# The FFNs' seven-product loop in a new order on VectorE and ScalarE, weight units' low parts on VectorE, and the products' weights 64 bytes off

## The chip, the cores and the metric

One core of one Trainium2 chip runs the whole kernel. The metric is device time in microseconds for one execution; smaller is better.

## The reference, cut to what matters

512 tokens of width 1024 pass through three layers in float32; each layer is a mixer and then an FFN. The mixers (pooling with dilated attention, retention, stick-breaking attention) are not touched by the change. The three FFNs have this form:

```python
def swiglu(h, w_in, w_out):
    gate, up = jnp.split(h @ w_in, 2, axis=-1)
    return (jax.nn.silu(gate) * up) @ w_out
```

The hidden width is 2816, 22 tiles of 128. Around an FFN stand an RMS norm of its input and the addition to the residual x.

## The kernel before, in words

**Products in two parts.** The result has float32 precision. Each float32 operand is split into a high part, rounded to fp32r, and a low part, the rest. A product is then three matmuls: high weights by high input, high by low, low by high. Everything is kept transposed: x is [128, 8 chunks, 512 tokens], and the weights are the stationary operand.

**Weight units.** A unit is the 8 chunks [128, 8, 128] that make one tile of 128 outputs. SP loads it into RAW (two slots, taken in turn), ScalarE (ACT) casts it to WH (`split_hi`, L374), GpSimd (POOL) takes WL = RAW - WH (`split_lo`, L645), and TensorE (PE) runs 16 matmuls of 512 columns on WH (`high_part`, L393 and L394) and 8 on WL (`low_part`, L402). SP starts the load two units on when the low part of a slot has been taken (`s_lo`); ACT's cast waits for the load (`s_raw`) and for PE to have used the slot's high part (`s_hi_used`); `s_unit` counts finished units.

**The FFN's up-projection.** Of the 22 hidden tiles, 14 (NC) are made by plain units, a gate unit and an up unit for each tile, into PSUM banks; VectorE (DVE) scales the gate by the norm RB (`gate_scaled`, L2158), ACT takes its silu, DVE scales the up part (L2162) and multiplies both (L2165). The other 8 (NS) are made by seven products in place of eight, as Strassen and Winograd do it: the 1024 x 2 tiles of weights (gate and up) and the 1024 x 512 input are cut in 2 x 2 blocks, and seven products of block sums (Q1, Q2, Q7, Q6, Q5, Q3, Q4 in the order of PE), each of 12 matmuls of 256 columns (L845, L847, L849), are added up in three half banks: a = B4, b = B5, c = B6. The sums of input blocks (TH, TL) are made once per FFN, those of weight blocks once per group, a group ahead.

**Opening.** PE runs four pairs of units (PRO = 4) while DVE makes the sums of the input (`input_sums`, L2172 to L2191, and their low parts, L2194 and L2198) and the first group's weight sums. In the first FFN the units 0 to 2 run inside the norm's update, and the banks of the pairs are given in the call (L2639). In the others, each pair writes B0 and B1 and so waits for the scaling of the pair before it (L816, L821). At its end DVE gives PE four credits for the banks (`sem_inc(t_bank, 4)`, L2309).

**The loop.** Eight iterations `seven(i)` follow on PE (L857), ACT (L1589) and DVE (L2236), each written out by hand in a fixed order. PE in one iteration: Q1, Q2, Q7, the high part of a gate unit, Q6, its low part, Q5, the high part of an up unit, Q3, Q4, its low part. In between PE waits for the low weights of each product (`t_lo`) and for banks that DVE has read (`t_bank`) or ACT has kept (`t_kept`: ACT copies a's partial sum after Q6 into CW). DVE copies a into GS and adds b (L2239, L2241), scales it (L2243), makes the sums for group i + 1 (L2208, L2212, L2216, L2219) and their low parts (`lo`, L2224), scales the plain gate, copies c into US (L2256) and subtracts a (L2258), which gives a back for Q3, and finishes the hidden tile (L2264 to L2271). ACT starts the loads of the next group's blocks (L1556 into SUMS7, L1557 into R), casts high parts and takes the silus.

**Tail.** The last two pairs of plain units run on PE while ACT and DVE split the finished hidden tiles HD into MH and ML (`some_hidden`; L1620 and L2280), which are the moving operands of the down projection. PE begins that when the last gate has been scaled; its first unit waits for each tile of M (L414 to L419).

**Memory.** Tensors are laid one behind the other in the order in which the code names them; `scratch` gives several lists the same place. A spacer PHASE of 128 bytes ahead of the scratch area makes MH, ML, SH7, SL7, TH and TL start at a multiple of 512 bytes. SH7 and SL7, the high and low weights of the seven products, stand first (each 28 x 128 elements), then TH. IDENT, the identity of the transposes, starts at 384 modulo 512.

## Time and profile before

| | |
|---|---|
| three executions | 2015.53, 2017.98, 2019.43 us; median 2017.98 |
| the profiled execution | 2017.78 us, its span 2016.0 us |
| PE busy | 1956.5 us (97%) in 9919 matmuls |
| DVE, ACT, POOL busy | 1172.7, 873.5, 663.5 us |
| chain that ended last | PE 73%, DVE 17%, DMA 5%, issue 3% |
| mean granted clock of TensorE | 0.992 |

Matmuls are pipelined and their records overlap, so a busy PE is not one at its peak: the distance from start to start says more than a matmul's own duration. A line of the trace has start, duration, engine, line of code, operation, output and inputs, and in brackets the idle time of the engine ahead of it with the instruction that ended it. DVEq is DVE's sequencer (an instruction without arithmetic). A row of a stretch has its bounds and length, each engine's busy time with the instructions in brackets, the granted clock of TensorE as a share of the full 2.4 GHz, the DMA engines' share and GB/s.

### The profile page before, as it was taken

How to read it: one execution, taken by the hardware profiler on the slowest of the kernel's cores; microseconds unless marked ns; L12 is line 12 of the kernel's file. 1: busy time of each engine (PE TensorE's matmuls, PEld its weight loads, DVE VectorE, ACT ScalarE, POOL GpSimd, SP SyncE). 2: the span in 40 equal slices, each digit the busy share in tenths (PEclk: the TensorE clock that was granted, in tenths of full speed). 3: DMA queues.
4: the chain of work that ended last, by engine and by line, in shares of the span. 5: the costliest groups of instructions: out<-in, count | busy, mean ns of one | idle time of the engine just before them, and what ended most of it. 6: DMA issues, size and time to landing. Idle time of an engine off the chain costs nothing.

```text
span 2016.0 us, 28330 instructions
## 1 busy us (share of the span) xinstructions
PE 1956.5 (97%) x9919; PEld 1635.1 (81%) x9919; DVE 1172.7 (58%) x1628; ACT 873.5 (43%) x1251; POOL 663.5 (33%) x259
## 2 busy tenths in 40 slices
PE   9999989999999999999999999999999999999999
PEld 6777778887888888888878888888777777888787
DVE  5765776767137456454277776324778777676600
ACT  6664533334234444434343334225888643232411
POOL 3233331214423334343442123443222243122443
PEclk9999989999999999999999999999999999999999
DMA  5212123222323222222332222322111132322222
GB/s 174 67 63 94 58 100 104 85 71 97 100 85 102 76 94 88 68 94 73 105 125 84 94 83 75 100 96 83 63 52 62 51 115 86 110 88 73 87 97 98
DMA packets 49023, 177.53 MB, mean 88 GB/s; under 512 B 5568, under 2 KB 6464, under 8 KB 48960
## 3 DMA queue, kind: packets, MB, share of 16 engines
q1 hardware_dynamic: 39744, 147.78, 22.2%
q10 hardware_dynamic: 9216, 28.91, 4.2%
q8 instruction: 40, 0.66, 0.1%
q14 instruction: 23, 0.19, 0.0%
HBM read 174.57 MB, written 2.10 MB: 88 GB/s over the span
## 4 chain that ended last, share of the span: by engine, by line
PE 73%; DVE 17%; DMA 5%; issue 3%; ACT 1%; DVEq 1%; ACTq 1%; SPq 0%
PE B L393 16%; PE B L394 16%; PE B L402 15%; DMA R<-in_w_seven 4%; DVE S L2216 3%; DVE HD L2165 2%; PE B L845 2%; DVE SL L2224 2%; PE B L849 2%; PE B L847 2%; DVE ML L2280 2%; PE B L1367 2%; PE B L414 1%; PE B L1175 1%; PE B L419 1%
## 5 line engine op out<-in xcount | busy, mean ns | idle before, releaser
L645 POOL TENSOR_TENSOR WL<-RAW,WH 128x1024 fp32r<-128x1024 f32 (+1 forms) x248 | 652.5, 2633 | 1324.9 <-PE B L402 835.5
L374 ACT CAST WH<-RAW 128x1024 fp32r<-128x1024 f32 (+1 forms) x252 | 278.6, 1107 | 636.0 <-PE B L394 558.5
L393 PE MATMUL B<-HH,WH 128*128 128x512 f32 x1224 | 482.1, 394 | 11.0 <-ACT WH L374 6.2
L394 PE MATMUL B<-HL,WH 128*128 128x512 f32 x1224 | 479.2, 392 | 0.0
L402 PE MATMUL B<-HH,WL 128*128 128x512 f32 x1224 | 304.8, 391 | 0.0
L393 PEld LDWEIGHTS B<-HH,WH 128*128 128x128 f32 x1224 | 231.2, 189 | 61.9 <-issue 8.7
L394 PEld LDWEIGHTS B<-HL,WH 128*128 128x128 f32 x1224 | 231.2, 189 | 46.3
L402 PEld LDWEIGHTS B<-HH,WL 128*128 128x128 f32 x1224 | 226.3, 188 | 45.6 <-POOL WL L645 0.4
L393 PE MATMUL B<-MH,WH 128*128 128x512 f32 x440 | 171.2, 389 | 0.0
L394 PE MATMUL B<-ML,WH 128*128 128x512 f32 x440 | 171.2, 389 | 0.0
L2328 DVE TENSOR_TENSOR X<-X,B 128x512 f32 x26 | 17.9, 687 | 206.7 <-PE B L402 192.9
L2140 DVE TENSOR_TENSOR ACC<-ACC,SQ 128x512 f32<-128x512 f32 x38 | 74.3, 1954 | 108.3 <-ACT SQ L1508 108.2
L845 PE MATMUL B<-HH,SH 128*128 128x256 f32 x288 | 86.5, 300 | 36.5 <-DVE SQ L2258 26.8
L847 PE MATMUL B<-TL,SH 128*128 128x256 f32 x384 | 109.0, 284 | 0.0
L849 PE MATMUL B<-TH,SL 128*128 128x256 f32 x384 | 109.0, 284 | 0.0
L845 PE MATMUL B<-TH,SH 128*128 128x256 f32 x384 | 108.9, 284 | 0.0
L1530 ACT ACTIVATE SG<-G 128x512 f32<-128x512 f32 x42 | 26.5, 631 | 188.5 <-DVE G L2158 188.4
L402 PE MATMUL B<-MH,WL 128*128 128x512 f32 x429 | 103.6, 389 | 0.0
L393 PEld LDWEIGHTS B<-MH,WH 128*128 128x128 f32 x440 | 82.6, 188 | 17.2
L394 PEld LDWEIGHTS B<-ML,WH 128*128 128x128 f32 x440 | 82.6, 188 | 17.1
L845 PEld LDWEIGHTS B<-HH,SH 128*128 128x128 f32 x288 | 57.6, 200 | 47.6 <-DVE SQ L2258 35.6
L402 PEld LDWEIGHTS B<-MH,WL 128*128 128x128 f32 x429 | 80.5, 188 | 16.7
(434 smaller groups left out, 3636.3 us busy)
## 6 DMA issues: line engine op xcount, KB each, us to landing
RAW<-in_w_small SPq DMA_DIRECT2D x206, 512.0 KB, 3.4
RAW<-in_w_large SPq DMA_DIRECT2D x48, 704.0 KB, 4.0
SUMS<-in_w_seven ACTq DMA_DIRECT2D x24, 512.0 KB, 4.0
R<-in_w_seven ACTq DMA_DIRECT2D x24, 512.0 KB, 4.8
out_t<-X SPq DMA_DIRECT2D x7, 256.0 KB, 5.1
X<-in_x_t ACTq DMA_DIRECT2D x4, 256.0 KB, 6.0
X<-in_x_t SPq DMA_DIRECT2D x4, 256.0 KB, 6.3
DECAY<-in_decay ACTq DMA_DIRECT2D x4, 256.0 KB, 2.6
```

What stands on the lines that cost most here:

```text
L374: act.copy(wh, raw).then_inc(s_hi, 1)
L393: pe.matmul(bank, wh[:, c, :], xh[:, k0 + c, :], start=(start and c == 0), stop=False)
L394: mm = pe.matmul(bank, wh[:, c, :], xl[:, k0 + c, :], start=False, stop=False)
L402: mm = pe.matmul(bank, wl[:, c, :], xh[:, k0 + c, :], start=False, stop=(stop and c == chunks - 1))
L645: pool.tensor_tensor(wl, raw, wh.bitcast(F32), ALU.subtract).then_inc(s_lo, 1)
L845: pe.matmul(bank, wh, xh[:, rows.start + c, cols], start=(start and c == 0), stop=False, skip_group_check=True)
L847: pe.matmul(bank, wh, xl[:, rows.start + c, cols], start=False, stop=False, skip_group_check=True)
L849: mm = pe.matmul(bank, wl, xh[:, rows.start + c, cols], start=False, stop=(c == 3), skip_group_check=True)
L1367: mm = pe.matmul(B[bank][:, o:o + w], weights, part[:, h, at:at + w], start=(start and n == 0), stop=(stop and n == 1), skip_group_check=True)
L2140: dve.tensor_tensor(ACC[:], ACC[:], SQ[b][:], ALU.add).then_inc(s_sq_used, 1)
L2165: dve.tensor_tensor(HD[:, i + NS, :], SG[:], U1[:], ALU.mult).then_inc(s_hidden, 1)
L2216: dve.tensor_tensor(S3[:], s6, A12, ALU.add).then_inc(t_sum, 1)
```

## The change

Five things.

1. Memory: TH (and TB22) come ahead of the weights, a spacer of 64 bytes follows (PHASE_SEVEN), then SH7, SL7 and SUMS7, which thus start at 64 modulo 512 bytes; further spacers bring what follows back to 0.
2. The low parts of the units 4 to 27 of every FFN are taken by DVE (`weights`) at written places, no longer by POOL, which waits meanwhile.
3. The loop's order on DVE and ACT; ACT makes the two PSUM copies; the low parts of Q4, Q3, Q6 and Q5 are made in the iteration that uses them.
4. The opening: pairs 1 to 3 of the second and third FFN use the banks (2, 3), (4, 5), (0, 1); the bank credits are given before the weight sums; loads of the first blocks start earlier. In the first FFN unit 7 uses B1.
5. The tail: the split of hidden tiles is spread otherwise.

```diff
-        MH, ML, G1, SG, U1, _, F = scratch([
-            ("MH", [P, FC, T], F32R), ("ML", [P, FC, T], F32R), ("G1", [P, T]), ("SG", [P, T]),
+        MH, _, ML, G1, SG, U1, _, F = scratch([
+            ("MH", [P, FC, T], F32R), ("PAST_MH", [P, 128]), ("ML", [P, FC, T], F32R), ("G1", [P, T]), ("SG", [P, T]),
...
-        SH7, SL7, TH, HD, _, S3, TL, R = scratch([
-            ("SH7", [P, 28, P], F32R), ("SL7", [P, 28, P], F32R), ("TH", [P, 16, T // 2], F32R), ("HD", [P, FC, T]),
+        TH, _, SH7, SL7, _, HD, _, S3, TL, R = scratch([
+            ("TH", [P, 16, T // 2], F32R), ("PHASE_SEVEN", [P, 16]), ("SH7", [P, 28, P], F32R), ("SL7", [P, 28, P], F32R),
+            ("PAST_SL7", [P, 112]), ("HD", [P, FC, T]),
...
POOL
+            by_vector = 2 * NC - 4
...
             for count, chunks in stretches:
+                if not chunks:
+                    first += count
+                    pool.wait_ge(s_lo, first)
+                    continue
...
PE, opening
                     use_unit(pe, Unit(u0 + 6), B[2][:], DC, HH, HL)
-                    pe.wait_ge(s_up, 1)
-                    use_unit(pe, Unit(u0 + 7), B[3][:], DC, HH, HL)
+                    pe.wait_ge(s_up, PRO - 1)
+                    use_unit(pe, Unit(u0 + 7), B[1][:], DC, HH, HL)
                 else:
                     pair(0, before)
-                    for n in range(1, PRO):
-                        pair(n)
+                    pe.wait_ge(s_gate, NC * f + 1)
+                    for n, bank in ((1, 2), (2, 4), (3, 0)):
+                        if n == 3:
+                            pe.wait_ge(s_up, NC * f + 1)
+                        use_unit(pe, Unit(u0 + 2 * n), B[bank][:], DC, HH, HL)
+                        use_unit(pe, Unit(u0 + 2 * n + 1), B[bank + 1][:], DC, HH, HL)
...
PE, loop: Q6 waits for t_lo + 5 (before: + 3), Q5 for + 6 (+ 4), Q3 and Q4 for none
...
ACT, loop
+                    act.wait_ge(t_lo, i * 6 + (6 * group0 + 3))
                     if produce:
-                        products_done(i, 2)
-                        act.wait_ge(t_lo, i * 6 + 6 * (group0 + 1))
-                        load(i + (group0 + 1))
+                        act.dma_start(R[:], blocks[i * 2 + (2 * group0 + 3)]).then_inc(t_landed_2, 16)
+                    products_done(i, 2)
+                    act.copy(GS[:, FIRST], B[5][:, FIRST]).then_inc(t_second, 1)
+                    if produce:
+                        act.dma_start(LANDED_1, blocks[i * 2 + (2 * group0 + 2)]).then_inc(t_landed_1, 16)
+                    products_done(i, 3)
+                    act.copy(US[:, SECOND], B[6][:, FIRST]).then_inc(t_seventh, 1)
                     split_hi(act, Unit(u0 + 2 * PRO + 2, i, 2), DC)
-                    if produce:
-                        singles_hi(ahead)
                     products_done(i, 4)
                     act.copy(CW, B[4][:, FIRST]).then_inc(t_kept, 1)
                     if produce:
+                        singles_hi(ahead)
                         sum_7_hi(ahead)
...
DVE, loop
+                def weights(u):
+                    dve.wait_ge(s_hi, u.index + 1)
+                    dve.wait_ge(s_unit, u.index - 1)
+                    raw, wh, wl = place(u)
+                    dve.tensor_tensor(wl, raw, wh.bitcast(F32), ALU.subtract).then_inc(s_lo, 1)
+
                 def seven(i, produce=True):
                     ahead = i + 1
-                    products_done(i, 2)
-                    dve.tensor_copy(GS[:, FIRST], a).then_inc(t_c11, 1)
-                    dve.wait_ge(t_c11, i * 2 + (2 * group0 + 1))
-                    dve.tensor_tensor(GS[:, FIRST], GS[:, FIRST], b, ALU.add).then_inc(t_bank, 1)
+                    lo(i, 6, Q4, A22)
+                    lo(i, 5, Q3, S3[:])
+                    up_and_hidden(i + (PRO - 1), B[1][:])
+                    dve.wait_ge(t_second, i + (group0 + 1))
+                    dve.tensor_tensor(GS[:, FIRST], GS[:, FIRST], a, ALU.add).then_inc(t_bank, 1)
+                    lo(i, 3, Q6, s6)
+                    weights(Unit(u0 + 2 * PRO, i, 2))
                     dve.wait_ge(t_bank, i * 4 + ((4 * NS + 4) * f + 5))
-                    dve.tensor_tensor(GS[:, FIRST], GS[:, FIRST], RB[:, FIRST], ALU.mult).then_inc(t_c11, 1)
+                    dve.tensor_tensor(GS[:, FIRST], GS[:, FIRST], RB[:, FIRST], ALU.mult).then_inc(t_first_half, 1)
+                    lo(i, 4, Q5, s5)
+                    weights(Unit(u0 + 2 * PRO + 1, i, 2))
...
                         sum_3(ahead)
+                    gate_scaled(i + PRO, B[0][:])
+                    if produce:
                         low_singles(ahead)
-                        lo(ahead, 2, Q7, s7)
-                    gate_scaled(i + PRO, B[0][:])
                     products_done(i, 5)
-                    dve.wait_ge(t_kept, i + (group0 + 1))
-                    dve.tensor_copy(US[:, SECOND], c_).then_inc(t_up, 1)
-                    dve.wait_ge(t_up, i + (group0 + 1))
+                    dve.wait_ge(t_seventh, i + (group0 + 1))
                     dve.tensor_tensor(US[:, SECOND], US[:, SECOND], a, ALU.subtract).then_inc(t_bank, 1)
                     if produce:
                         minus_sum_5()
-                        lo(ahead, 3, Q6, s6)
-                        lo(ahead, 4, Q5, s5)
+                        lo(ahead, 2, Q7, s7)
...
-                    up_and_hidden(i + PRO, B[1][:])
-                    if produce:
-                        lo(ahead, 5, Q3, S3[:])
-                        lo(ahead, 6, Q4, A22)
...
DVE, opening and tail
+                opening_gate(0)
+                opening_up(0)
                 input_sums()
-                opening_pair(1)
+                opening_gate(1)
+                dve.wait_ge(s_lo, u0 + 4)
+                weights(Unit(u0 + 4))
+                opening_up(1)
+                weights(Unit(u0 + 5))
                 input_sums_lo()
-                opening_pair(2)
+                opening_gate(2)
+                weights(Unit(u0 + 6))
+                opening_up(2)
+                dve.sem_inc(t_bank, 4)
                 sum_7(0)
                 sum_6(0)
                 sum_3(0)
                 minus_sum_5()
+                weights(Unit(u0 + 7))
                 low_singles(0)
                 lo(0, 2, Q7, s7)
...
-                opening_pair(3)
-                dve.sem_inc(t_bank, 4)
+                opening_gate(3)
...
+                end = u0 + 2 * (NC - 2)
+                weights(Unit(end))
+                up_and_hidden(NC - 3, B[1][:])
+                weights(Unit(end + 1))
+                some_hidden(range(0, 5))
                 gate_scaled(NC - 2, B[0][:])
-                some_hidden(range(0, 5))
+                weights(Unit(end + 2))
+                some_hidden(range(5, 9))
                 up_and_hidden(NC - 2, B[1][:])
-                some_hidden(range(5, 14))
+                weights(Unit(end + 3))
+                some_hidden(range(9, 12))
                 gate_scaled(NC - 1, B[0][:])
-                some_hidden(range(14, 18))
+                some_hidden(range(12, 19))
                 up_and_hidden(NC - 1, B[1][:])
-                some_hidden(range(18, FC))
+                some_hidden(range(19, FC))
```

ACT's opening loads the first blocks ahead of pair 1, and casts unit 8 between the singles and the sums; its tail follows the same spread of hidden tiles (0 to 4, 5 to 8, 9 to 11, 12 to 18, 19 to 21).

## Rows read from the trace of the kernel before

**Rows 1.** The page's first line.
```profile
span 2016.0 us, 28330 instructions
```

**Rows 2.** The page's groups by line: busy, mean ns of one | idle before, releaser.
```profile
L845 PE MATMUL B<-HH,SH 128*128 128x256 f32 x288 | 86.5, 300 | 36.5 <-DVE SQ L2258 26.8
```

**Rows 3.** Stretches (openings, loops, tails): length, busy PE PEld DVE ACT POOL, PEclk, DMA.
```profile
240.25:272.65 32.40, 21.99 (x81) 16.95 (x80) 29.71 (x42) 17.56 (x27) 9.87 (x5) 0.88 0.24 82
1021.75:1048.58 26.83, 22.53 (x97) 17.86 (x96) 24.77 (x29) 14.81 (x21) 11.83 (x5) 1.00 0.30 102
1657.42:1685.69 28.27, 22.53 (x98) 17.87 (x97) 26.48 (x29) 14.73 (x21) 10.05 (x4) 0.99 0.33 115
272.65:454.08 181.43, 172.86 (x1056) 154.75 (x1057) 119.36 (x164) 54.45 (x82) 39.23 (x16) 0.98 0.27 90
1048.58:1229.51 180.93, 171.74 (x1057) 153.62 (x1057) 119.23 (x164) 54.55 (x82) 39.86 (x16) 0.99 0.27 90
1685.69:1867.60 181.91, 172.88 (x1056) 154.77 (x1057) 119.16 (x164) 54.55 (x83) 39.97 (x16) 0.98 0.26 87
454.08:478.10 24.02, 21.93 (x98) 17.84 (x96) 20.00 (x21) 11.22 (x19) 11.34 (x4) 1.00 0.33 111
1229.51:1253.51 24.00, 21.92 (x97) 17.84 (x95) 19.97 (x21) 11.21 (x19) 11.33 (x4) 1.00 0.34 112
1867.60:1891.60 24.00, 21.92 (x97) 17.84 (x95) 19.99 (x21) 11.21 (x19) 11.34 (x4) 1.00 0.33 113
```

**Rows 4.** Timeline of PE, first matmul of Q3 in the second FFN's third iteration.
```profile
1112.23 0.38 PE L845 MATMUL B<-HH,SH 128*128 128x256 f32 x1 [1.40 <-DVE SQ L2258]
```

**Rows 5.** Timeline of DVE in the same iteration.
```profile
1104.62 0.69 DVE L2208 TENSOR_TENSOR SUMS<-SUMS,R 128x512 f32<-128x512 f32 x1 [4.35 <-DMA R<-in_w_seven]
...
1106.07 2.77 DVE L2216 TENSOR_TENSOR S<-SUMS 128x512 f32<-128x512 f32 x1
1108.97 1.83 DVE L2224 TENSOR_TENSOR SL<-SUMS,SH 128x1024 fp32r<-128x1024 f32 x2
...
1111.76 0.42 DVE L2258 TENSOR_TENSOR SQ<-SQ,B 128x256 f32<-128x256 f32 x1
```

**Rows 6.** Timeline of POOL in the same iteration.
```profile
1105.83 2.46 POOL L645 TENSOR_TENSOR WL<-RAW,WH 128x1024 fp32r<-128x1024 f32 x1 [8.78 <-PE B L402]
```

**Rows 7.** Timeline of PE, last iteration of the first FFN: start, 37th matmul, last low part.
```profile
433.04 0.28 PE L845 MATMUL B<-HH,SH 128*128 128x256 f32 x1
...
437.36 0.40 PE L393 MATMUL B<-HH,WH 128*128 128x512 f32 x1
...
452.24 2.00 PE L402 MATMUL B<-HH,WL 128*128 128x512 f32 x8
```

**Rows 8.** The page's DMA issues: KB each, median us to landing.
```profile
RAW<-in_w_small SPq DMA_DIRECT2D x206, 512.0 KB, 3.4
...
R<-in_w_seven ACTq DMA_DIRECT2D x24, 512.0 KB, 4.8
```

**Rows 9.** Timeline of PE, first product of the second FFN.
```profile
1048.58 0.38 PE L845 MATMUL B<-HH,SH 128*128 128x256 f32 x1 [2.06 <-DVEq L2309]
```

**Rows 10.** Timeline of DVE, opening of the first FFN.
```profile
249.04 0.68 DVE L2158 TENSOR_TENSOR G<-B,RB 128x512 f32<-128x512 f32 x1
```

**Rows 11.** Timeline of DVE, tail of the first FFN.
```profile
466.69 10.76 DVE L2280 TENSOR_TENSOR ML<-HD,MH 128x512 fp32r<-128x512 f32 x9
```

**Rows 12.** Timeline of PE, first matmul of the first down projection.
```profile
478.10 0.50 PE L414 MATMUL B<-MH,WH 128*128 128x512 f32 x1 [2.09 <-DVE G L2158]
```

**Rows 13.** One more such stretch, from 1.4 us after the second FFN's tail.
```profile
1254.90:1258.20 3.30, 3.30 (x10) 2.52 (x9) 3.19 (x6) 3.30 (x6) 0.00 (x0) 0.50 0.02 5
```

**Rows 14.** Groups by line in two windows of 30 ns, 1105.57 and 1106.88 on.
```profile
L845 PE MATMUL B<-TH,SH 128*128 128x256 f32 x1 | 0.3, 277 | 0.0
...
L845 PE MATMUL B<-TH,SH 128*128 128x256 f32 x1 | 0.3, 283 | 0.0
```

**Rows 15.** Timeline of PE, transposes in the attention of the first layer.
```profile
165.67 1.25 PE L1019 MATMUL B<-IDENT,PR 128*128 128x128 f32 x10
```

More of the change, by code:

```diff
@@ L888, in ffn @@
                 pe.wait_ge(t_input_lo, 4 * (f + 1))
+                pe.wait_ge(s_up, NC * f + PRO - 1)
                 with pe.Fori(0, NS) as i:
@@ L1629, in ffn @@
                 input_block()
+                load(group0)
                 pair(1, DC, splits[1])
-                load(group0)
                 input_sums_hi()
                 pair(2, DC, splits[2])
-                for hi in (singles_hi, sum_7_hi, sum_6_hi, sum_5_hi, sum_3_hi, single_4_hi):
+                singles_hi(0)
+                split_hi(act, Unit(u0 + 2, 3, 2), DC)
+                for hi in (sum_7_hi, sum_6_hi, sum_5_hi, sum_3_hi, single_4_hi):
                     hi(0)
-                pair(3, DC, splits[3])
+                silu(3)
+                split_hi(act, Unit(u0 + 3, 3, 2), DC)
                 with act.Fori(0, NS - 1) as i:
@@ L1640, in ffn @@
                 products_done(NS - 1, 7)
-                pair(NC - 2, DC, between=lambda: some_hidden(range(0, 10)))
-                some_hidden(range(10, 14))
-                pair(NC - 1, chunks_after, between=lambda: some_hidden(range(14, EARLY)))
-                some_hidden(range(EARLY, FC))
+                some_hidden(range(0, 5))
+                pair(NC - 2, DC, between=lambda: some_hidden(range(5, 9)))
+                some_hidden(range(9, 12))
+                pair(NC - 1, chunks_after, between=lambda: some_hidden(range(12, 19)))
+                some_hidden(range(19, FC))
             def outputs(o, n, u0, per, chunks, chunks_after, gain_next=None, begun=False):
@@ L2285, in some_hidden, with opening_gate, opening_up @@
                         hidden_lo(t)
[L2287 to L2295 removed]
+                banks = banks or ((0, 1), (2, 3), (4, 5), (0, 1))
+                def opening_gate(n):
+                    gate_scaled(n, B[banks[n][0]][:])
+                def opening_up(n):
+                    up_and_hidden(n, B[banks[n][1]][:])
+                opening_gate(0)
+                opening_up(0)
+                input_sums()
+                opening_gate(1)
[3 more added lines that the diff above has]
+                weights(Unit(u0 + 5))
                 input_sums_lo()
[L2297 removed]
+                opening_gate(2)
+                weights(Unit(u0 + 6))
+                opening_up(2)
+                dve.sem_inc(t_bank, 4)
                 sum_7(0)
```

47 lines of the change are left out of this document (21 added, 26 removed).

## The prediction

> **What bounds the kernel now.** The profiled execution took 2017.78 us, of which its span is 2016.0 us [rows 1]; the median of the three runs is 2017.98 us, so sums made against this profile hold for the median to 0.2 us. I read the page first: TensorE (PE) has the matmuls of the three FFNs on the path, and the one large group whose engine sat idle before it is L845, the products of the seven-product loop, released by DVE L2258 [rows 2]. Second, I cut each FFN into opening, loop and tail by the starts of its products: openings (from the point where their order will differ) of 32.40, 26.83 and 28.27 us, loops of 181.43, 180.93 and 181.91 us, tails of 24.02, 24.00 and 24.00 us [rows 3]. PE is never the one that others can catch up with; what counts is where it waits inside these nine stretches.
>
> In the loop it waits once per iteration, before the third A-product (Q3), for 1.40 us in the iteration shown [rows 4], and so in all 21 iterations that prepare a next group. DVE is late there because of this chain: the blocks' DMA lands (4.35 us of idle DVE), three sums, the low part of the singles, the gate's scaling, and only then the copy and the subtraction that free bank a at 1111.76 + 0.42 [rows 5]. One sum in it (L2216) takes 2.77 us where the same shape just before takes 0.69: it starts inside POOL's low part of a weight unit, 1105.83 to 1108.29 [rows 6], and ends after it. In all three openings PE waits for the bank credit that DVE gives last (L2309), and in the tails for the last gate's scaling (L2158), which stands behind nine low parts of hidden tiles.
>
> **The loop.** The change moves both unit low parts from POOL to DVE, moves two PSUM copies (L2239, L2256) from DVE to ACT, and reorders DVE so that nothing of the next group stands before what the running group needs. The last iteration of an FFN prepares no next group and shows the cost without the wait: it starts at 433.04 and the loop ends at 454.08, 21.04 us; its first 36 products take 437.36 - 433.04 = 4.32 us, 120 ns each, so seven products are 10.08 us and the two units the other 10.96, of which a low part is 1.84 [rows 7]. Counted from an iteration's start, PE needs: Q6's weights at 8.0, the gate's low part at 9.4, Q5's weights and CW at 11.25, bank a for Q3 at 16.3, the up unit's low part at 19.2. DVE after the change, at 1.15 us for 1024 elements, 0.6 for 512 and 0.4 for 256 (estimates: the pair 1024 + 512 takes 1.83 and 256 alone 0.42 [rows 5]) and some 0.2 more where one waits for the last one's result, beginning at 0.5 when the group before is done: two low parts and a hidden tile until 3.5, the sum in GS until 3.95, Q6's low part to 4.6, the gate unit's low part to 5.8, Q5's to 6.8, the up unit's to 8.0; the subtraction for Q3 runs right after product 5, at about 13.5. Every one is over 2 us early. DVE's list adds to some 15.5 of 21 us, so it isn't the bound by 5 us an iteration; the two new operations cost it 2.3 us, the removed copies give 0.8 back, and POOL's lock no longer stretches two of its sums. ACT gets the two half-bank copies, some 0.4 us each (DVE's subtraction of that shape takes 0.42 [rows 5]), beside PE's products. Its two block loads are no longer issued together: R's goes out at 1.3, the singles' at 3.9, and both have landed before DVE wants them at 8.0. POOL stands at a wait through the whole loop. SP's unit loads now follow DVE's low parts: the gate unit's RAW is free at 5.8, a load lands in 3.4 us [rows 8], ACT casts until 10.3, copies CW until 10.7: 0.5 us early, the thinnest margin. So I cost the loop at 24 x 21.04 = 505.0 us against 544.3: **-39.3 us**.
>
> **The openings.** In FFN 2 and 3 the new bank plan lets PE run units 2 to 7 without asking for a scaled gate each time. From the start of unit 4's turn, 1021.75 and 1657.42, four units follow at 5.45 us each (a tail's 21.93 us of PE busy, less the 0.16 by which the last matmul's record runs over [rows 3]), 21.8 us, against 26.83 and 28.27: **-5.0 and -6.5**. PE's wait on the bank credit (2.06 us in FFN 2 [rows 9]) goes because the credit is given before the weight sums. DVE must deliver unit 4's low part by 1025.4; after the input sums (5.9 us as in FFN 1, with POOL's lock gone for most of them) and gate 1 it has it near 1022.5. FFN 1 is different. Of its 32.40 us PE is busy for 21.99 [rows 3]; POOL's low part of unit 4 is ready where it begins, at 240.25. On DVE that low part will stand behind gate 1's scaling, which starts at 249.04 [rows 10]: ready at 250.85, and PE idles 10.6 us at a stretch instead of in three shorter pieces. Then it has four units less a high part to do, some 18 us, up to 3.4 us more by slow clock, and one short wait for unit 6: a first product between 271.1 and 272.9, against 272.65; DVE's own list (sums, unit 7, singles) ends at 270.1. I take **-1.0**, ends -1.6 and +0.3.
>
> **The tails.** DVE held the last gate's scaling behind nine hidden low parts, 10.76 us, stretched by POOL [rows 11], and PE waited 2.09 us [rows 12]. With the new split of hidden tiles gate 13 is scaled 5 us before it is asked for, so a tail is 21.8 us: **-6.6** in all. What is late next is hidden tile 21, ready some 6 us before its matmul. After these waits in FFN 2 and 3 the granted clock was at its lower level, 0.50 (1.2 GHz), for a stretch of 3.4 us [rows 13]; half of that is lost, 1.7 us each; with no wait before it I let it go: **-3.4**, ends 0 and -3.4. POOL's queue opens again with DVE's last unit low part, some 14 us into a tail, before ACT's cast of the next unit (about 16) lets it work at all.
>
> The sum is 39.3 + 5.0 + 6.5 + 1.0 + 6.6 + 3.4 = 61.8 us, and 2017.78 - 61.8 = 1956.0.
>
> **The 64 bytes.** This is a cost that no row shows. Counted from the tensor sizes in the code, the weights and the moving operands of the products all start at 0 modulo 512 bytes now; after the change the weights start at 64. Rows do show that a weight load and a running matmul disturb each other: a product behind a 512-column matmul takes 277 ns, all later ones 283 [rows 14], at otherwise the same work. The nearest row with operands at different phases is the transposes' (moving IDENT at 384 modulo 512, weights PR at 0): ten in 1.25 us with 0.27 for the last, so (1.25 - 0.27)/9 = 109 ns apart [rows 15], the least that any weight load and matmul of this kernel keep between them. That is the lower end: 120 to 109, times 7 x 12 x 24 = 2016 products, is 22 us less. The upper end is by the worst such disturbance, those 6 ns once more: 12 us more. I take nothing in the forecast, since one shift of 64 bytes within streams that both sweep over all 512 bytes need not move the meeting, and these ends come into the range. The Trainium skill (TensorE: Matmul & The Clock Gate, "What happens when you issue a matmul") says that PE has two independent SBUF read ports and that a weight load steals nothing from the running matmul; by that the shift is worth exactly zero. The trace's 277 against 283 ns speaks against it being quite exact.
>
> **The rivals.**
> (a) The shift helps: products at 113 to 109 ns, 14 to 22 us less, 1942 to 1934. For it: the 277/283 rows and the 109 of the transposes. Against: those transposes move 128 columns for each load, the products 256. The Trainium skill's TensorE page ("Back-to-back issue gap") has N/2.4 + 2.5 ns between matmuls, 109 for 256 columns, and by it the time would also be 1934; the 120 ns of these rows don't follow it.
> (b) A new wait takes the old one's place: CW is copied behind ACT's cast of the next gate unit, which waits for a load that can no longer start before DVE's low part at 5.8. Each us that this load lands past the 0.5 us of margin stops PE before Q5 in 21 iterations. If the three loads crowd and it takes the 4.8 us that R takes [rows 8] instead of 3.4, the wait is 0.9 us, 19 us in all: 1975. With products at 109 ns half of the margin is gone too, so (a) and (b) together end near 1950.
> (c) Slower than before: the shifted weights collide with every moving stream. It decides where a product goes from 120 to 151 ns (61.8/2016 = 31 ns); if each product waited out a load of its own, 109 ns by [rows 15], it would be 229 ns and 2176 us. The disturbance that [rows 14] show is 6 ns, a fifth of what this needs.
> (d) The shift isn't there, because some tensor's size rounds otherwise: then the forecast holds unchanged.
>
> **How the numbers follow.** A measurement of this kernel can tell about 0.2% (4 us) from no change. Forecast, with (d): 0.45, own range 1948 to 1966. (a), with its mixture with (b): 0.33. (b) alone or with a slightly worse product: 0.18. (c): 0.03, and 0.01 for landing near 2018. The range takes (a)'s lower end and (b)'s price: 1934 to 1975, about 2 in 10 outside. Faster by over 0.2%: 0.96; within: 0.01; slower: 0.03.
>
> **What would show it.** In the new trace: no idle before Q3's first product; an iteration of 21.04 us start to start; DVE's L2216 sum at 0.69 us everywhere and POOL idle in the FFN loops; openings of 21.8 us in FFN 2 and 3 and a hole of over 10 us in FFN 1's; no wait before the down projection; products 120 ns apart with 283 ns each. A wait of PE before Q5 with ACT's CW copy as releaser is (b); 113 ns or less between products is (a); over 125 is (c)'s direction. I am wrong in kind if an iteration is longer than 22 us.

## The result, and the profile after

The changed kernel takes **1956.59 us** (median of 4 runs, 1955.05 to 1957.99) against 2018.01 us (4 runs) of the kernel before on the same chip: a ratio of 0.9697, 95% interval 0.9680 to 0.9714. The forecast was 1956.0 us. The profiled execution took 1957.37 us, 60.4 less than that of before, where the working gave 61.8. A total that fits can be made of terms that don't, so the stages come first.

The first lines of the page after come here. In the page's row of PE for 40 equal slices of the execution every slice is at least 90% busy but one, the opening of the first FFN, and POOL has lost 184 us of work.

```profile
span 1955.6 us, 28150 instructions
PE 1934.5 (99%) x9919; PEld 1622.4 (83%) x9919; DVE 1120.2 (57%) x1652; ACT 892.8 (46%) x1299; POOL 479.8 (25%) x187
```

The page's chain is now PE 93%, DVE 3%, DMA 2%; DVE had 17% of it before. The nine stretches that answer to [rows 3], with the same columns:

```profile
240.25:271.11 30.86, 20.40 (x82) 16.33 (x81) 26.19 (x40) 16.18 (x25) 0.00 (x0) 0.83 0.28 92
1005.38:1027.14 21.76, 21.76 (x97) 18.02 (x96) 18.75 (x25) 14.51 (x21) 0.00 (x0) 1.00 0.32 100
1621.31:1643.07 21.76, 21.76 (x98) 18.02 (x96) 18.74 (x25) 14.51 (x21) 0.00 (x0) 1.00 0.30 97
271.11:440.23 169.12, 167.73 (x1058) 150.79 (x1057) 111.33 (x171) 63.81 (x104) 0.00 (x0) 1.00 0.30 95
1027.14:1197.34 170.20, 168.12 (x1057) 150.70 (x1056) 109.97 (x168) 62.14 (x102) 0.00 (x0) 1.00 0.29 92
1643.07:1811.19 168.12, 167.32 (x1058) 150.79 (x1056) 109.62 (x168) 62.12 (x102) 0.00 (x0) 1.00 0.29 94
440.23:461.99 21.76, 21.76 (x98) 18.02 (x97) 19.64 (x27) 13.24 (x23) 3.25 (x1) 1.00 0.38 124
1197.34:1219.10 21.76, 21.76 (x97) 18.02 (x96) 19.65 (x27) 13.24 (x23) 3.25 (x1) 1.00 0.37 122
1811.19:1832.95 21.76, 21.76 (x98) 18.02 (x96) 19.64 (x27) 13.24 (x23) 3.25 (x1) 1.00 0.39 125
```

The sum of each kind, against [rows 3]:

| stage | before | after | gain | forecast |
|---|---|---|---|---|
| three loops | 544.27 | 507.44 | 36.8 | 39.3 |
| opening, FFN 1 | 32.40 | 30.86 | 1.5 | 1.0 |
| openings, FFN 2 and 3 | 55.10 | 43.52 | 11.6 | 11.5 |
| three tails | 72.02 | 65.28 | 6.7 | 6.6 |
| all the rest (whole less these) | 1313.99 | 1310.27 | 3.7 | 3.4 |

The loops are off by 2.5 us, the other stages by 0.5 or less. Nor is the loops' gain one thing. The waits before Q3, counted as the distance between two matmuls beyond an undisturbed one, were 30.2 us in all before, and they are gone. With them went 2.3 us behind them: after a wait the second product started 222 to 224 ns after the first, not 120. Another 6.9 us were the granted clock. Each loop of before began with a stretch at the lower level (1.2 GHz), behind the wait that ended its opening (2.06 us in the second FFN [rows 9]), and its products were 213 ns apart there. Two of these stretches:

```profile
1050.00:1053.40 3.40, 3.40 (x19) 3.40 (x18) 0.42 (x1) 0.00 (x0) 0.72 (x1) 0.50 0.64 231
1684.90:1691.70 6.80, 6.02 (x28) 6.02 (x29) 1.13 (x3) 0.88 (x1) 2.38 (x1) 0.50 0.28 102
```

So nearly a fifth of what the table puts down to the loops was earned in front of them. After the change all three loops run at the full clock.

FFN 2's loop still takes 2.1 us more than FFN 3's at the same number of matmuls. PE waits in it before Q5's first product in three iterations (in two of FFN 3, three of FFN 1). Here are the timelines of PE, of DVE, of SP's queue and of ACT in one of them:

```profile
1121.32 2.00 PE L404 MATMUL B<-HH,WL 128*128 128x512 f32 x8
1123.83 0.39 PE L857 MATMUL B<-TH,SH 128*128 128x256 f32 x1 [0.52 <-ACT SQ L1613]
```
```profile
1116.83 1.22 DVE L2260 TENSOR_TENSOR WL<-RAW,WH 128x1024 fp32r<-128x1024 f32 x1
```
```profile
1118.23 2.38 SPq L569 DMA_DIRECT2D RAW<-in_w_small  x2
```
```profile
1122.46 1.05 ACT L376 CAST WH<-RAW 128x1024 fp32r<-128x1024 f32 x1 [5.64 <-DMA RAW<-in_w_small]
1123.42 0.36 ACT L1613 COPY SQ<-B 128x256 f32<-128x256 f32 x1
```

That is rival (b), link by link: DVE's low part (L2260) frees RAW, SP issues the load, ACT's cast waits for it, and CW (the program's name in the trace is SQ, L1613) is copied behind the cast. The load took 4.2 us from issue to cast where the forecast had 3.4. In the eight waits of this kind the two matmuls are 0.24 to 0.98 us further apart than undisturbed ones, 5.6 us in all.

The loads themselves have changed. These are the times from issue to landing of SP's unit loads in the second FFN's loop, 16 of them, first before and then after the change:

```profile
DMA to landing us min/median/max: 3.3/3.4/3.5
```
```profile
DMA to landing us min/median/max: 3.4/4.1/4.4
```

Before, all 48 unit loads of the three loops landed within 3.6 us. Now the gate unit's load goes out 3 us behind the load into SUMS7 and 2 us ahead of the up unit's. It took 4.1 to 4.5 us in the eight waits and 3.3 to 3.6 us in the other 16 iterations, the three last ones, which load no blocks, among them (3.3 to 3.5). That the loads slow each other is what this suggests; no run moves one of them alone.

Beside rival (b) a part of rival (a) has come true: most products are 117 to 118 ns apart, no longer 120 [rows 7], and their records last 281 ns, no longer 283 [rows 14]. In Q5, the product behind these waits, 128 of the 1908 distances are even shorter, 113 or 114 ns, in iterations with a wait and without. The products' forms by tile (minimum, median, maximum in ns):

```profile
L857 PE MATMUL B<-TH,SH x384: 276/281/388, 273.9 to 1809.0; 128*128 128x256 f32 x192
L857 PE MATMUL B<-HH,SH x288: 281/281/282, 271.1 to 1807.6; 128*128 128x256 f32 x144
```

The first FFN's hole is where it was forecast, and longer than any wait of before. PE stops after the high part of unit 4, whose low part DVE makes behind gate 1:

```profile
240.20 0.40 PE L396 MATMUL B<-HL,WH 128*128 128x512 f32 x1
251.05 2.50 PE L404 MATMUL B<-HH,WL 128*128 128x512 f32 x5 [10.46 <-DVE WL L2260]
```
```profile
249.19 0.68 DVE L2178 TENSOR_TENSOR G<-B,RB 128x512 f32<-128x512 f32 x1
249.79 1.21 DVE L2260 TENSOR_TENSOR WL<-RAW,WH 128x1024 fp32r<-128x1024 f32 x1
```

Two stretches by window follow. The granted clock falls to the lower level (0.51, 1.2 GHz) from 4 us into the hole until 4 us behind it. It is full behind the second tail, where [rows 13] had 0.50; PE no longer waits there.

```profile
244.90:255.10 10.20, 4.05 (x10) 3.24 (x11) 8.62 (x17) 1.06 (x2) 0.00 (x0) 0.51 0.30 104
1220.40:1223.80 3.40, 3.40 (x16) 2.82 (x16) 3.40 (x2) 0.77 (x2) 3.40 (x1) 1.00 0.07 26
```

### The profile page after: what moved, and what is told of

It reads as the page before. It is cut to its first block, busy times and chain, and to the rows that moved or that the text cites. A ratio compares the mean times of both kernels' runs of the same rounds, so it can differ in the third digit from the quotient of the medians.

```text
span 1955.6 us, 28150 instructions
## 1 busy us (share of the span) xinstructions
PE 1934.5 (99%) x9919; PEld 1622.4 (83%) x9919; DVE 1120.2 (57%) x1652; ACT 892.8 (46%) x1299; POOL 479.8 (25%) x187
## 4 chain that ended last, share of the span: by engine, by line
PE 93%; DVE 3%; DMA 2%; issue 1%; ACT 1%; DVEq 0%; SPq 0%; ACTq 0%
PE B L395 21%; PE B L396 21%; PE B L404 20%; PE B L857 3%; PE B L861 3%; PE B L859 3%; DMA RAW<-in_w_small 2%; PE B L1378 2%; PE B L1186 1%; PE B L1190 1%; PE B L1187 1%; PE B L416 1%; PE B L421 1%; PE B L417 1%; PE B L1367 1%
## 5 line engine op out<-in xcount | busy, mean ns | idle before, releaser
L647 POOL TENSOR_TENSOR WL<-RAW,WH 128x1024 fp32r<-128x1024 f32 (+1 forms) x176 | 468.8, 2667 | 1448.1 <-PE B L404 1053.1
L404 PE MATMUL B<-HH,WL 128*128 128x512 f32 x1224 | 306.7, 393 | 10.5 <-DVE WL L2260 10.5
L2260 DVE TENSOR_TENSOR WL<-RAW,WH 128x1024 fp32r<-128x1024 f32 x72 | 87.7, 1218 | 0.4
L2244 DVE TENSOR_TENSOR SL<-SUMS,SH 128x1024 fp32r<-128x1024 f32 (+1 forms) x96 | 78.2, 818 | 6.1 <-ACT SH L1571 6.1
L857 PEld LDWEIGHTS B<-TH,SH 128*128 128x128 f32 x384 | 72.1, 188 | 10.7 <-ACT SQ L1613 8.9
```

Of the source, the lines that this page charges most:

```text
L404: mm = pe.matmul(bank, wl[:, c, :], xh[:, k0 + c, :], start=False, stop=(stop and c == chunks - 1))
L647: pool.tensor_tensor(wl, raw, wh.bitcast(F32), ALU.subtract).then_inc(s_lo, 1)
L857: pe.matmul(bank, wh, xh[:, rows.start + c, cols], start=(start and c == 0), stop=False, skip_group_check=True)
L2244: dve.tensor_tensor(SL7[:, form, :], x, SH7[:, form, :].bitcast(F32), ALU.subtract).then_inc(t_lo, 1)
L2260: dve.tensor_tensor(wl, raw, wh.bitcast(F32), ALU.subtract).then_inc(s_lo, 1)
```

## The experiments

The theory after the first look: the order of the work gives the gain, and the loops are 505.0 us at 120 ns, less what the 64 bytes give, plus rival (b)'s waits. Three questions stand against it: are the two corrections really these; does the gain come from POOL's lock rather than from the order; can the 64 bytes do more or less elsewhere. Each edit below is against the changed kernel unless said otherwise.

### The two corrections

**no_shift**: the spacer is 512 bytes, so the products' weights are back at 0 (what lies behind them moves along and stays at 0).

```diff
-            ("TH", [P, 16, T // 2], F32R), ("PHASE_SEVEN", [P, 16]), ("SH7", [P, 28, P], F32R), ...
+            ("TH", [P, 16, T // 2], F32R), ("PHASE_SEVEN", [P, 128]), ("SH7", [P, 28, P], F32R), ...
```

> The changed kernel with the spacer ahead of SH7 at 512 bytes in place of 64, so that the seven products' weights start at 0 modulo 512 again; all else is as changed. Theory A (the 64 bytes make a product shorter by some 2.3 ns, 120 to 117.7): products are 120 ns apart, each 283 ns, and the time is 1956.6 + 2016 x 0.0023 = about 1961 us. Rival B (the shorter products come from the new order of tensors or of the loop, not from the phase): products stay near 117.7 ns, the time at 1956 to 1957 us. Under A the waits before Q5 should be rarer or shorter too, because PE comes there 0.2 us later in each iteration.

Measured: 1959.71 us (1958.66 to 1959.88, 5 runs), ratio 0.9704 [0.9691, 0.9718]. The products are 120 ns apart again. PE still waits before Q5, over 0.2 us in six iterations, 2.95 us in all. So the 64 bytes are worth some 3 us net by the medians. In the two traces the loops differ by 1.9 us (509.31 against 507.44). They give more than that at the products, 3.8 us by the next runs, and some of it comes back as rival (b)'s waits. A faster PE reaches Q5 sooner, but only by 0.1 us in an iteration (11.15 and 11.24 us after its start); the gate unit's load took over 4 us eight times in the one trace and five times in the other, and that can be chance.

**cw_first**: ACT copies CW before it casts the next gate unit.

```diff
-                    split_hi(act, Unit(u0 + 2 * PRO + 2, i, 2), DC)
                     products_done(i, 4)
                     act.copy(CW, B[4][:, FIRST]).then_inc(t_kept, 1)
+                    split_hi(act, Unit(u0 + 2 * PRO + 2, i, 2), DC)
```

> The changed kernel with ACT copying the partial sum CW ahead of its cast of the next gate unit. Theory A (PE's waits before Q5, 5.6 us in eight iterations, are the copy standing behind a cast that waits for a late load): no wait before Q5 is left and the time falls by 4 to 6 us, to 1951 to 1953. Rival B (the load is late anyway and the wait only moves to the next gate unit's high part, or the later cast delays the casts of the singles): the same time within 1.5 us, with a wait at another place.

Measured: 1951.78 us (1951.09 to 1957.31, 5 runs), ratio 0.9672 [0.9656, 0.9688], 4.8 us below the changed kernel. Theory A holds: no wait is left in any of the 24 iterations, though five of the gate unit's loads still took 4.2 us or more, and the loops are equal to the last digit. Its windows, and the timeline of ACT, where the load is still waited for (0.73 us), but by nothing that PE needs:

```profile
272.04:439.08 167.04, 167.04 (x1058) 151.38 (x1057) 110.04 (x169) 63.33 (x104) 0.00 (x0) 1.00 0.30 94
1026.12:1193.16 167.04, 167.04 (x1057) 151.37 (x1056) 109.75 (x168) 62.53 (x102) 0.00 (x0) 1.00 0.30 94
1638.94:1805.98 167.04, 167.04 (x1057) 151.37 (x1056) 109.57 (x168) 62.25 (x102) 0.00 (x0) 1.00 0.29 94
```
```profile
1119.15 0.37 ACT L1612 COPY SQ<-B 128x256 f32<-128x256 f32 x1 [4.70 <-PE B L861]
1120.25 1.05 ACT L376 CAST WH<-RAW 128x1024 fp32r<-128x1024 f32 x1 [0.73 <-DMA RAW<-in_w_small]
```

The three loops are 501.12 us, 6.3 less than the changed kernel's 507.44. That is rival (b)'s price. The trace of the changed kernel has its parts: 5.8 us of waits (the eight and three shorter ones), 1.2 us for second products that come 221 to 226 ns behind the first instead of 118, less 0.6 us for the distances of 113 and 114 ns, 6.4 us in all.

**cw_256**: cw_first, and the products' weights at 256 modulo 512 (spacers of 64 and 64 elements in place of 16 and 112).

> CW ahead of the cast (as in cw_first, 1951.8) and the products' weights at 256 modulo 512 in place of 64. Theory A (what counts is how the two streams meet; at 0 products are 120 ns apart, at 64 117.7, in two of the runs 113 after another entry): some other value than 117.7, between 113 and 125, the time moving by 2.0 us per ns. Rival B (any value but 0 gives the same 117.7): 1951.8 within 1.5 us.

Measured: 1955.36 us (1955.09 to 1957.88, 4 runs), ratio 0.9684 [0.9665, 0.9704]; products at 120 ns. One loop's window:

```profile
1027.04:1195.36 168.32, 168.32 (x1058) 152.61 (x1057) 109.53 (x168) 62.29 (x102) 0.00 (x0) 1.00 0.29 93
```

168.32 is 8 x 21.04, the forecast's iteration, to the last digit; three such loops are 504.96. The 64 bytes are thus worth 504.96 less 501.12, 3.8 us, and 3.84/2016 is 1.9 ns for each product. Its theory B (any value but 0 gives 117.7 ns) fails: 256 is as slow as 0. With this the loops close: 505.0 less 3.8, and 6.4 more by the parts of rival (b)'s price, are 507.6, against 507.44 measured.

### The order, or POOL's lock

**low_on_pool**: POOL takes all the unit low parts as before; DVE's `weights` does nothing, and its one wait on `s_lo` in the opening goes too; all else is as changed.

```diff
-            cuts = [..., (by_vector, 0), (14, HALF), (2, HALF), (6, DC)]
+            cuts = [..., (by_vector, DC), (14, HALF), (2, HALF), (6, DC)]
...
                 def weights(u):
-                    dve.wait_ge(s_hi, u.index + 1)
-                    ...
+                    pass
```

> The changed kernel with POOL taking the low parts of all plain units again, as in the kernel before; DVE takes none; order, banks, copies and the 64 bytes stay. Theory A (the gain is the order: nothing of the next group stands before what the running group needs, and DVE has over 5 us of slack an iteration to be stretched by POOL's lock): the loop stays near 169 us a time, DVE's L2236 sum is stretched to 2 us and more again, PE does not wait before Q3; FFN 1's hole of 10.6 us is gone or smaller, and the time is 1950 to 1958. Rival B (the gain is the lock that is gone): waits of PE in the loop come back with 1 us an iteration, the time is 1975 or more.

Measured: 1954.4 us (1953.43 to 1956.95), ratio 0.9679 [0.9660, 0.9699]. The median is 2.2 us below the changed kernel's, but the runs of both overlap, so this says not slower, and no more; what follows is read from the stages. The stretching is all there again. One loop's window with POOL's 16 low parts, two operations of DVE that ran beside them (the like take 1.23 and 0.69 us after the change), and one group by line, whose mean of 1216 ns is 692 in the changed kernel (one of its like took 2.77 us in [rows 5]):

```profile
1025.37:1193.03 167.66, 167.32 (x1057) 151.32 (x1057) 120.05 (x156) 65.26 (x105) 39.48 (x16) 1.00 0.28 95
```
```profile
1100.06 2.92 DVE L2244 TENSOR_TENSOR SL<-SUMS,SH 128x1024 fp32r<-128x1024 f32 x1
...
1109.82 2.42 DVE L2244 TENSOR_TENSOR SL<-R,SH 128x512 fp32r<-128x512 f32 x1 [0.41 <-DVE HD L2296]
```
```profile
L2236 DVE TENSOR_TENSOR S<-SUMS 128x512 f32<-128x512 f32 x24 | 29.2, 1216 | 0.8
```

And yet PE waits only three times in its loops (0.50, 0.28 and 0.24 us), each time before Q3, where the kernel before waited too. The timeline of PE at the first of them:

```profile
1146.58 0.38 PE L857 MATMUL B<-HH,SH 128*128 128x256 f32 x1 [0.34 <-DVE SQ L2284]
```

The loops are 502.3 us in all, 42.0 below the kernel before. Of these, 6.9 are the clock at the loops' start and 3.8 the 64 bytes. The other 31 us are the waits before Q3 with what stood behind them, and since POOL's work is all there, the new order of DVE and ACT is enough to remove all but 1.0 us of these waits. Moving the low parts to DVE adds 1.2 us at best (501.12 with CW first) and costs 5.1 as the change has it (507.44), where RAW is freed only when DVE comes to it: POOL has the gate unit's low part 2.7 us into most iterations, DVE 5.6 to 6.1 us.

In FFN 2 and 3 the openings have a wait of 1.6 us each with POOL, so there DVE is the better place. In FFN 1 it is the worse one: with POOL the hole of 10.5 us is three shorter waits of 6.8 us in all, and the first product comes at 269.75 instead of 271.11. Whether DVE's low parts in the old order would have gained anything was not tried.

**old_tail**: cw_first, with the hidden tiles spread over ACT and DVE as in the kernel before (0 to 4 after gate 12, 5 to 13 ahead of gate 13), and DVE's low parts beside them.

```diff
-                some_hidden(range(0, 5))
                 gate_scaled(NC - 2, B[0][:])
+                some_hidden(range(0, 5))
...
-                some_hidden(range(9, 12))
+                some_hidden(range(5, 14))
                 gate_scaled(NC - 1, B[0][:])
```

> The version with the CW copy first, with the old spread of the 24 hidden tiles over ACT and DVE (DVE again has the low parts of its units at the end of the loop, the new lock on POOL stays away). Theory A (the wait before the down projection came from the lock between DVE and POOL): the wait stays away, 1951.8 us. Theory B (it came from the place of the hidden tiles' operations in the order): the three waits return at 6.6 us in all, with up to 3.4 us of slow clock behind them, 1955 to 1962 us, and the gaps stand in front of the down projection's first matmul with DVE or ACT named.

(An FFN has 22 hidden tiles, not the 24 of this text.)

Measured: 1951.61 us (1951.56 to 1952.41, 4 runs), ratio 0.9676 [0.9657, 0.9695], the same as cw_first. Theory A holds. The nine low parts of [rows 11] take half as long, 5.50 us instead of 10.76, and the gate behind them is scaled in time. DVE's and PE's timelines:

```profile
452.97 5.50 DVE L2303 TENSOR_TENSOR ML<-HD,MH 128x512 fp32r<-128x512 f32 x9
458.39 0.69 DVE L2177 TENSOR_TENSOR G<-B,RB 128x512 f32<-128x512 f32 x1
```
```profile
460.35 0.39 PE L416 MATMUL B<-MH,WH 128*128 128x512 f32 x1
```

So in the tail it is the other way round: taking POOL off is enough, and the new spread is not needed once that is done. low_on_pool, which has the new spread and POOL's stretching, shows tails of 21.76 us too: either cure alone removes the whole wait.

### The bytes

**before_shift**: the kernel before, with the new memory layout and nothing else.

> The kernel before with the new memory layout alone (TH ahead, the products' weights at 64 modulo 512), its order untouched. Theory A: its products too fall from 120 to about 117.7 ns; the loop's wait before Q3 is timed by DVE and takes most of that back, since DVE's chain starts from the block loads and PE only gains in front of a wait, so the time falls by 1 to 4 us, to 2014 to 2017. Rival B (phase without effect): 2018, products at 120 ns.

Measured: 2019.0 us (2012.47 to 2021.44, 10 runs), ratio 1.0001 [0.9988, 1.0014]: no difference, where theory A had 1 to 4 us. The products are at 117 to 118 ns, and at 113 to 114 in Q3 and Q4 behind the wait (most of 367 such among 1807 distances). But the wait before Q3 is timed by DVE, and PE waits longer by what it gains: 35.5 us before Q3 in the three loops, 30.2 before. One loop's window (PE is busy for 168.32 of 179.79 us; before, 171.74 of 180.93 [rows 3]):

```profile
1053.25:1233.04 179.79, 168.32 (x1057) 150.25 (x1057) 119.10 (x164) 54.80 (x82) 40.03 (x16) 1.00 0.27 91
```

The other two loops end longer than before (182.57 and 183.70 us). Three of their waits, of 1.8 us each, are followed by a stretch at the lower clock, where none of the waits before Q3 in the kernel before was. In the loop shown, waits of 1.8 us are not followed by one, so what decides stays open.

**cw_448** and **cw_128**: cw_first with the products' weights at 448 and at 128.

> As cw_256 with the products' weights at 448 modulo 512, that is 64 bytes behind the moving operands in place of ahead. Theory A: a value of its own; if it is mirrored, above 120 (over 1956 us). Rival B: 117.7 and 1951.8 within 1.5 us.

> The version with the CW copy first, with the weights of the seven products at 128 bytes modulo 512. So far the product matmuls start 120 ns apart at 0 and at 256, 117.7 at 64 and 117.5 at 448. Theory A (any place off the multiples of 256 bytes does it): 117.5 to 118 ns, 1951 to 1952 us. Theory B (the distance to a multiple of 128 bytes decides): 120 ns, some 4.7 us more, 1955 to 1957 us.

Measured, at 448 and at 128: 1949.64 us (1949.06 to 1950.18), ratio 0.9652 [0.9634, 0.9671], and 1955.41 us (1955.14 to 1956.13), ratio 0.9694 [0.9675, 0.9713]. One loop of each:

```profile
1025.12:1191.52 166.40, 166.40 (x1057) 151.16 (x1056) 109.50 (x168) 62.48 (x102) 0.00 (x0) 1.00 0.30 94
```
```profile
1026.44:1194.92 168.48, 168.48 (x1057) 152.46 (x1056) 109.56 (x168) 62.25 (x102) 0.00 (x0) 1.00 0.29 93
```

A loop takes 168.32 us at 256, 168.48 at 128, 167.04 at 64, 166.40 at 448. At 128 theory B of its expectation holds: being off the multiples of 256 is not enough, 128 is as slow as 0 and 256. (The products there are 119.4 ns apart in the mean, now 115 and now 124.) At 448 the products are as far apart as at 64, 117.8 ns in the mean of both traces. What 448 gives more is at the 512-column matmuls: of the units' 1292 low-part matmuls 914 are followed after 226 or 227 ns at 64 and 1049 at 448, and 57 and 15 after 236 ns. Neither theory of its expectation holds whole: the value is not above 120 ns, and the time is over 1.5 us below 1951.8.

**unit_weights_64**: WH and WL of the plain units start at 64 as well.

```diff
+        sb("PHASE_WEIGHTS", [P, 16])
         WH = [sb(f"WH{s}", ...
...
-        sb("PHASE", [P, 32])
+        sb("PHASE", [P, 16])
```

> The changed kernel with WH and WL, the weights of all plain units, 64 bytes further too (IDENT, MEANR, ACC and SQ move along by 64). Theory A (the phase matters only where a weight load is as long as its matmul, in the 256-column products): matmuls of 512 columns stay 226.7 ns apart and the time is that of the changed kernel within 2 us. Rival B (every weight load that meets its matmul's stream at another phase costs less): they fall by up to 2 to 5 ns, times some 7000 that is 14 to 35 us less. Rival C: they rise.

Measured: 1986.66 us (1985.95 to 1987.88), ratio 0.9841 [0.9826, 0.9856]: 30 us slower than the changed kernel. The tail, which is plain units only, and PE in it:

```profile
441.18:463.58 22.40, 22.40 (x98) 18.05 (x96) 19.79 (x27) 13.36 (x22) 3.24 (x1) 1.00 0.39 123
```
```profile
441.18 0.39 PE L396 MATMUL B<-HH,WH 128*128 128x512 f32 x1
441.41 0.40 PE L397 MATMUL B<-HL,WH 128*128 128x512 f32 x1
441.65 0.39 PE L396 MATMUL B<-HH,WH 128*128 128x512 f32 x1
```

Rival C holds. 22.40 against 21.76 us is 0.64 over 96 matmuls, 6.7 ns each. Over the whole trace the 512-column matmuls on WH and WL, some 6300, are 5.5 ns further apart than in the changed kernel, 35 us in all, and the products gave 7 us back: they fell to 113 to 114 ns everywhere but in the first eleven products of FFN 3 and in parts of some Q5s. The two make 28 of the 29 us by which the traces differ. So the same shift that gives a 256-column matmul 2 ns takes 6 from a 512-column one, and the products' distance depends on more than the place of their own weights: on that of the matmuls around them, or on how PE comes to them, as in Q5 of the changed kernel. (This edit also moves IDENT and the tensors behind it.)

### The opening of the first FFN

**opening**: cw_first, and in the first FFN POOL takes units 4 and 5, DVE unit 6's low part comes first and pairs 1 and 2 ahead of the input sums' low parts; ACT casts units 6 and 7 earlier. The branch for the other FFNs stays.

```diff
                 opening_up(0)
+                if f == 0:
+                    dve.wait_ge(s_lo, u0 + 6)
+                    weights(Unit(u0 + 6))
+                    input_sums()
+                    opening_gate(1)
+                    opening_up(1)
+                    opening_gate(2)
+                    opening_up(2)
+                    weights(Unit(u0 + 7))
+                    input_sums_lo()
```

> CW ahead of the cast, and in FFN 1 alone POOL takes the low parts of units 4 and 5, ACT casts unit 6 and 7 ahead of the silus they stood behind, and DVE takes unit 6's low part first and finishes pairs 1 and 2 before the input sums' low parts. Theory A (the first product of FFN 1 is set by DVE's list of some 22 us from its first scaling on, which becomes 2.3 us shorter and no longer waits for casts): PE's hole at 240 us is gone, the first product comes at 265 to 267 in place of 271.1, less 1.7 to 3.4 us of slow clock behind the hole that moves to its front: 1947 to 1950 us. Rival B (the sums wait for the block loads or ACT's casts of the input sums): the first product stays at 270 to 271 and the time at 1951 to 1953.

Measured: 1946.73 us (1946.29 to 1947.07, 5 runs), ratio 0.9638 [0.9622, 0.9653], a little better than theory A's 1947 to 1950. The first product comes at 264.88 instead of cw_first's 272.04 (0.9 us of this are cw_first's longer stretch at the lower clock behind the hole, 13.7 us where the changed kernel, with the first product at 271.11, had 10.2); 1.9 of these 7.2 us are given back, since PE now waits right ahead of the loop and starts it at the lower clock (168.98 us for the loop, not 167.04). DVE's list has lost two low parts (2.4 us) and a wait of 3.0 us for ACT's cast of the input sums. What bounds the opening now is the list itself, on which DVE works without a pause from 243.5 us on. PE's timeline and one window at the loop's start:

```profile
257.72 1.97 PE L404 MATMUL B<-HH,WL 128*128 128x512 f32 x8
264.88 0.58 PE L857 MATMUL B<-HH,SH 128*128 128x256 f32 x1 [5.19 <-DVE SL L2248]
```
```profile
264.90:271.70 6.80, 6.80 (x39) 6.71 (x40) 4.93 (x9) 2.71 (x5) 0.00 (x0) 0.69 0.32 100
```

**opening_448**: opening with the weights at 448.

> The opening version with the weights of the seven products at 448 bytes modulo 512 instead of 64. Theory A (the two edits are apart: 448 gave 2.1 us over 64 in the pair of runs with the CW copy first, 1951.78 to 1949.64, and the opening gave 5.05 us, 1951.78 to 1946.73): 1944.6 us. Theory B (with the opening mended, the products of FFN1 run into a DVE or ACT wait that the faster products only uncover): 1946.7 us, the gain eaten, and a wait of over 1 us stands in FFN1's loop.

Measured: **1945.36 us** (1944.65 to 1945.92, 5 runs), ratio 0.9643 [0.9627, 0.9659] against the runs of before beside it (2018.43). The later two loops are at 166.40 us, the first product at 265.12, and the first loop at 169.10. It lies 1.4 us below opening, between the two theories and nearer to the one of separate gains. It is the fastest version found, 11 us below the changed kernel and 73 below the kernel before.

## Why the prediction was right, and where it was so by luck

- **The loop at 24 x 21.04 us.** This was right as a mechanism and, at 120 ns a product, exact: cw_256 has three loops of 168.32. The last iteration of [rows 7] was a true picture of one without waits. Reading an undisturbed instance in the same trace was worth more than any estimate of the parts. It also took in what the prediction didn't see: it speaks of waits before Q3 in all 21 iterations, but the first of each FFN waits only 0.2 us, and 6.9 of the 39.3 us are the lower clock at the loops' start. The undisturbed iteration held both, so the sum was right without this.
- **The thinnest margin.** The forecast named the link (RAW freed at DVE's low part, load, ACT's cast, CW) and 0.5 us of margin, and then took the wait at nothing. The step that was wrong is the load's 3.4 us [rows 8]. This was the time of a load in the old order, in which all 48 unit loads of the loops landed in 3.3 to 3.6 us. In the new order 29 of the 48 took over 3.9 us, and the gate unit's 4.1 to 4.5 us in the eight waits. The margin was also thinner than 0.5 us: RAW was free at 5.6 to 6.1 us, not 5.8, the load was issued 0.2 us after that, and PE asked for Q5 at 11.15, not 11.25. Rival (b) had the mechanism, with 4.8 us for the load in all 21 iterations and 19 us; it came in 8 iterations and cost 6.3 us.
- **The 64 bytes at nothing.** Mis-sized: 1.9 ns for each product, 3.8 us. It lay near the zero end of the range from -11 to +6 ns. The 109 ns of the transposes, rival (a)'s lower end, was reached by no version. The 113 ns was: in stretches of the changed kernel and of before_shift, and nearly throughout in unit_weights_64. The 277 against 283 ns of [rows 14], from which the prediction has it that weight load and matmul disturb each other, are lengths of records whose ends are modelled; they don't show it by themselves.
- **Luck in the total.** The two terms left out, -3.8 and +6.3, nearly cancel. The other stages gained 1.1 us more than forecast, and the median lies 0.8 us below the profiled execution, so 1956.0 stands 0.6 us from 1956.59 although the loops are 2.5 us off.
- **POOL's lock.** The forecast counted it as a part of the cause ("stretches two of its sums"). The stretching was real, and in the loop's new order it has next to no weight: low_on_pool has all of it back and 1.0 us of waits. What it cost in the old order was not measured. In the tails, with the old spread, taking POOL off was enough by itself.
- **The openings.** FFN 2 and 3 took 21.76 us, forecast 21.8. What the new banks did there, and what the earlier credits, was not tried apart. In **FFN 1** the low part was forecast at 250.85 and was ready at 251.00; PE's hole was forecast at 10.6 us and is 10.46; the first product came at 271.11, the early end of 271.1 to 272.9.
- **The tails** took 21.76 (21.8), and **the slow clock** behind the second and third is gone: 3.7 us for all the rest, forecast 3.4.
- **Rival (c)** had 120 to 151 ns as its point; no product came near. But the direction exists: the plain units' matmuls lose 6.7 ns in the tails of unit_weights_64, as large as the upper end taken from [rows 14].

## What to carry to other kernels

Where a loop has an iteration that prepares nothing, it shows the price of the others without their wait: use it. A load's median time holds for the order in which it was measured. When a change lets the load start beside others, the margin behind it must bear the longer time as well (here 4.1 to 4.5 us instead of 3.4). Ask also what stands in the queue behind the instruction that waits for the load, and put there only what may be late.

Before work is moved off an engine because it disturbs another, see whether the disturbed operations are on the path in that stage. Here they were in the tail. In the loop they were not once the order was new, and the reordering did almost all that the move was thought to do.

A wait at the end of one stage can be paid for in the next, by a clock that is low at its start: cut a trace into stages with the clock beside them before a gain is put down to a stage.

## What the runs showed of the hardware

The distance between back-to-back matmuls with a new weight load each depends on the byte at which their weights start, at otherwise the same instructions. The byte is counted from the sizes in the code, modulo 512, with the moving operands at 0; that 512 is the period was not tested. With 256 columns the mean is 119.6 ns at 256, 119.4 at 128, and 117.8 at 64 and at 448, where nothing waits. Stretches of 113 to 114 ns came at 64, mostly behind waits, and nearly throughout with the other weights shifted as well. With 512 columns and weights at 0, five in six distances are 226 to 227 ns; with them at 64, most are 230 to 236.

The Trainium skill (TensorE: Matmul & The Clock Gate, "What happens when you issue a matmul") has two independent SBUF read ports and a weight load that steals nothing from the running matmul, by which the place of the weights should not count; here it counts, by 2 ns in 120 and 6 in 227. The same page of the Trainium skill ("Back-to-back issue gap") gives N/2.4 + 2.5 ns for an isolated matmul at the full clock, 109 ns for 256 columns, which the products reached in no version. What in the memory or the port makes the difference is open; no run here isolates one load and one stream.
